# Sample projections in plain fp32 in four column groups from refetched raw weights; the convolution's current-token tap taken by ScalarE from PSUM

## The chip, the core and the metric

One core of one Trainium2 chip runs the whole kernel as one program. The metric is the device time in microseconds (us) of one execution. TensorE (PE) multiplies, VectorE (DVE), ScalarE (ACT) and GpSimd (POOL) do the elementwise work, and SyncE (SP) issues the DMAs, all of them on one queue. Each engine executes its own instruction list in order and waits for the others by semaphores.

## What is computed

One layer of a decoder trunk, for 2048 prompt tokens and for 8 sample tokens (one new token of each of 8 sequences), with the same weights. Everything is fp32.

```
h    = rms_norm(x) * (1 + scale) + shift           # width 1024
proj = h @ w_in                                    # u_a, z_a, q k v, z_b, gates
y_a  = pool_mix(u_a) * silu(z_a)                   # causal pooling, windows 2 4 8 16
q,k,v = silu(causal_conv(qkv))                     # 4 taps per channel
o    = gated delta rule(q, k, v, beta, g)          # chunked for the prompt, one step for the sample
y    = concat(y_a, rms_norm(o) * silu(z_b)) @ w_out
out  = x + gate * rms_norm(y)
```

The convolution of token i is x[i-3]*w[0] + x[i-2]*w[1] + x[i-1]*w[2] + x[i]*w[3]. The part of it that this case touches is the last tap, that of the current token.

## The kernel before

The prompt is worked in four blocks of 512 tokens. In each block PE goes through 24 projection tiles of 128 output channels (tiles 0 to 11 are k, q and v, tiles 12 to 23 are z and u) and then 8 output tiles. Every big product is made of three fp32r products, high x high, high x low and low x high, so a projection tile is 24 matmuls of 128x128 by 128x512 (`tile`, lines 2128 to 2130) into one of two PSUM accumulators, `acc[t % 2]`. Tile t may start when the reader of tile t-2 has emptied that accumulator (`tile_reader`).

The weights come raw from memory only in block 0. There SP loads 256 KB halves into three buffers `wraw`, ACT rounds each half to fp32r (the high part, L901), POOL or DVE subtracts (the low part, L1900), and SP stores the finished 1 MB tile to the DRAM copy `kept`. Blocks 1 to 3 load those 1 MB tiles from `kept` into one of three slots `wsl` (`load_tile`, L739): the load of tile t+3 waits until PE has finished tile t. Since SP runs one list, every wait of SP delays what stands behind it.

A q, k or v tile is convolved after PE: ACT copies the accumulator to `raw` (L934). DVE multiplies `raw` with the first tap into `cacc` (`convolve`, L1248) and adds the other three taps, each with one scalar_tensor_tensor (L1251). ACT then takes the silu into `cq` (L993) and, for q and k, the square into `tmpa` (L1001). `cacc` has two buffers. Between the convolutions DVE builds the gate rows (gg, L1643, which needs ACT's logarithm L1032) that PE waits for behind tile 3, the decay matrices, and from tile 8 on a forward substitution in 31 pairs of small operations (L1333, L1336), before and between the readers of tiles 12 and 13 (L1367).

The 8 sample tokens ride along in block 3, the last one. Ahead of each projection tile PE computes the same 128 channels for them (`sample_tile`): the normed rows are the stationary operand, as fp32r, 16 columns wide (high and low parts of 8 rows, `hs2`), and the tile of weights, already in its slot `wsl`, is the moving one; 16 matmuls of 128 columns (L2204, L2205). ACT copies the 16 rows to `spt`, and after each four tiles PE turns them with four transposes (`sample_join`, L2215) and DVE adds high and low (L1384) into `pj`. From there the sample's convolution, state step and output follow in small steps that ride in the slots behind the projection tiles.

Of the kernel before, what the change touches and what calls it, by code (L numbers as in the profile page):

```python
# [283 lines left out]
def sample_out_steps():  # L284
# [14 lines left out]
    "dve": (["xn", "h0", "h", "hh", "hl"] + ["g_a", "pg0", "g_beta", "g_sp", "g_g", "pg1", "g_d0", "g_d1"] + sample_plan_steps() + sample_out_steps() + ["ys1", "yn", "yr"]),  # L299
# [3 lines left out]
def layer_kernel(nc, a):  # L303
    ctx = ExitStack()
    with ctx:
# [62 lines left out]
        spt = over("spt", rw, 0, [2 * NS, WR, BT])  # L368
# [31 lines left out]
        hs2 = sb("hs2", [P, KT, 2 * NS], F32R)  # L400
# [29 lines left out]
        fold = sb("fold", [GR * BS, 1 + NS])  # L430
# [15 lines left out]
        hs = sb("hs", [P, KT, NS])  # L446
# [113 lines left out]
        raw_f, hist_in, hist_out = event("raw_f", NQ), event("hist_in", NQ), event("hist_out", NQ)  # L560
        conv_a, conv, silu = event("conv_a", 3 * NQ), event("conv", NQ), event("silu", NQ)
# [103 lines left out]
        def tile_reader(eng, it, t):  # L665

            t = t - 2
            if t < 0:
                eng.wait_ge(*ytok_f(it, t - 2))
            elif t < NQ:  # L670
                eng.wait_ge(*raw_f(it, t))
# [16 lines left out]
        def _(sp):  # L688
# [51 lines left out]

            def y_rows(it):

                for t in range(4):
                    sp.wait_ge(*yr_f(it, t))
                    sp.dma_start(a["y"][it, t], ytok[:, t]).then_inc(y_out.sem, 16)
# [17 lines left out]
            def block_of(it, last=False):  # L763
                enter(it)
                if last:
                    sp.wait_ge(*h_hi(it, -1))
                    sp.wait_ge(*h_lo(it, -1))
                    for dst, src in ((cbuf, a["s_conv"]), (pbuf, a["s_pool"])):
                        sp.dma_start(dst[:], src).then_inc(sm_st, 16)
                    sp.dma_start(ssm[:], a["s_ssm"]).then_inc(sm_ssm, 16)  # L770

                for t in range(NW):
                    if it == 0:
                        split_tile(t)
# [99 lines left out]
        def _(act):  # L874
# [96 lines left out]
            def sample_tile(it, t):  # L971

                g, j = divmod(t, 4)
                act.wait_ge(*done("pe", f"sp{t}"))
                if t == 0:
                    act.wait_ge(*split_done(NW - 1, 1))
                if j == 0 and g >= WR:
                    act.wait_ge(*done("pe", f"sc{g - WR}"))
                nc.scalar.activation(spt[:, g % WR, j * P:(j + 1) * P], bank("sp", t)[0:2 * NS, 0:P], ACT.Copy).then_inc(*step("act", f"pj{t}"))
# [166 lines left out]
        def _(dve):  # L1146
# [7 lines left out]
            nc.vector.memset(ones[:], 1.0)  # L1154
            nc.vector.memset(hot[:], 0.0).then_inc(s_pad, 1)
# [84 lines left out]
            def convolve(it, t):  # L1240
# [4 lines left out]
                dve.wait_ge(*raw_f(it, t))  # L1245
                dve.wait_ge(*hist_in(it, t))
                dve.wait_ge(*silu(it, t - 2))
                nc.vector.tensor_scalar(cacc[:, t % 2], r[:, 0:BT], cw[:, t, 0:1], None, ALU.mult).then_inc(conv_a.sem, 1)  # L1248
                for j in range(1, CK):
                    dve.wait_ge(*conv_a(it, 3 * t + j - 1))  # L1250
                    nc.vector.scalar_tensor_tensor(out=cacc[:, t % 2], in0=r[:, j:j + BT], scalar=cw[:, t, j:j + 1],  # L1251
                                                   in1=cacc[:, t % 2], op0=ALU.mult, op1=ALU.add
                                                   ).then_inc((conv_a if j < CK - 1 else conv).sem, 1)
# [121 lines left out]
            def sample_join(it, g):  # L1375
# [4 lines left out]
                turned = bank("sc", g)[:, 0:8 * NS].rearrange("p (t e s) -> p t s e", e=2, s=NS)  # L1380

                def join(to, tiles):

                    return nc.vector.tensor_reduce(pj[:, to:to + tiles.stop - tiles.start], turned[:, tiles], AX.X, ALU.add)  # L1384
# [177 lines left out]
            def sample_rows():  # L1562

                dve.wait_ge(*done("pe", "hs"))
                nc.vector.tensor_tensor(hs[:], row_bank[:, 0:64].rearrange("p (k s) -> p k s", k=KT), amul[:, :, 1:1 + NS],
                                        ALU.mult).then_inc(*step("dve", "h0"))
                dve.wait_ge(*done("dve", "h0"))
                nc.vector.tensor_tensor(hs[:], hs[:], mod[:, 0:8, 1:1 + NS], ALU.add).then_inc(*step("dve", "h"))
                dve.wait_ge(*done("dve", "h"))
                nc.vector.tensor_copy(hs2[:, :, 0:NS], hs[:]).then_inc(*step("dve", "hh"))  # L1570
                dve.wait_ge(*done("dve", "hh"))
                nc.vector.tensor_tensor(hs2[:, :, NS:], hs[:], hs2[:, :, 0:NS].bitcast(F32), ALU.subtract).then_inc(*step("dve", "hl"))
# [19 lines left out]
            def block_of(it, last=False):  # L1592
                enter(it)
                for t in range(NQ):
# [434 lines left out]
        def _(pe):  # L2029
# [15 lines left out]
            def turn_rows(j):  # L2045

                pe.wait_ge(s_rows, j + 1)
                for i in range(4):
                    last = nc.tensor.matmul(turn_bank[j // 2][:, 36 * (j % 2) + 9 * i:36 * (j % 2) + 9 * (i + 1)],
                                            rows96[j][:, i * P:(i + 1) * P], fold[:], start=True, stop=True)  # L2050
# [159 lines left out]
            def sample_join(it, g):  # L2210
# [77 lines left out]
            def block_of(it, last=False):  # L2288
                enter(it)
                for t in range(NQ):  # L2290
                    if last:
                        if t == 0:
                            pe.wait_ge(*done("dve", "hl"))
# [147 lines left out]
def layouts(i):  # L2441
# [5 lines left out]
    def tiles(w):  # L2447
# [20 lines left out]
        "fold": np.tile(np.concatenate([np.eye(1 + NS), np.zeros((BS - 1 - NS, 1 + NS))]), (GR, 1)).astype(np.float32),  # L2468
# [64 lines left out]
```

## Time and profile before

| what | value |
|---|---|
| median of 3 runs | 1063.57 us (1062.31 to 1066.26) |
| profiled execution | 1062.29 us, of it the span of the trace 1060.5 us |
| PE busy | 1017.0 us, 96% of the span |
| DVE, ACT, POOL busy | 669.1, 363.8 and 218.0 us |
| DMA moved | 202.32 MB |
| block 3 begins | 768.81 us after the start |

PE is busy almost throughout, so the columns to look at are how long each piece of its work occupies it (from one start to the next, since matmuls overlap) and the few places where it waits. The other engines' busy time matters only at those places.

### The profile page before, as it was taken

Reading aid. Unit: us, or ns where it says so; the run is one execution under the profiler, and the core shown is the slowest. Engines: PE = TensorE matmul, PEld = TensorE weight load, DVE = VectorE, ACT = ScalarE, POOL = GpSimd, SP = SyncE. Lnnn points to the kernel's source line nnn. Section 1 sums busy time; section 2 is a strip of 40 time slices with the busy share of each in tenths; the row PEclk is TensorE's granted clock in tenths of the full one; section 3 lists DMA queues with packets and bytes.
Section 4 is the critical chain, followed back from the end, with each engine's and each line's share of the span. In section 5 each row is a group of like instructions: output and inputs, shape, how many; then the busy total and the mean of one; then the engine's idle time right before and its main releaser. Section 6 shows DMA issues by size and latency. Waiting matters only on the chain.

```text
span 1060.5 us, 16761 instructions
## 1 busy us (share of the span) xinstructions
PE 1017.0 (96%) x6235; PEld 796.3 (75%) x6235; DVE 669.1 (63%) x1392; ACT 363.8 (34%) x725; POOL 218.0 (21%) x222
## 2 busy tenths in 40 slices
PE   4999989999999999999999999999999999999995
PEld 1567667877777788887877788887877888888774
DVE  2479897577356795566356884676256775555644
ACT  5356322433714511322524511314426531121211
POOL 0133345565400101231000102230000100533000
PEclk9989999999999999999999999999999999999998
DMA  9696566364867553243756553244674343322265
GB/s 344 250 363 230 207 221 269 123 221 160 294 223 269 197 195 128 112 159 132 265 184 252 199 198 120 80 178 160 258 283 169 119 159 120 115 80 86 95 233 179
DMA packets 46803, 202.32 MB, mean 191 GB/s; under 512 B 9162, under 2 KB 9930, under 8 KB 29188
## 3 DMA queue, kind: packets, MB, share of 16 engines
q1 hardware_dynamic: 46724, 201.26, 51.8%
q8 instruction: 50, 0.82, 0.3%
q14 instruction: 29, 0.24, 0.1%
HBM read 156.43 MB, written 44.81 MB: 190 GB/s over the span
## 4 chain that ended last, share of the span: by engine, by line
PE 66%; DVE 1%; issue 1%; POOL 1%; ACT 0%; DVEq 0%; POOLq 0%; ACTq 0%
PE acc L2128 13%; PE acc L2130 12%; PE acc L2129 12%; PE ring L2178 9%; PE ring L2165 2%; PE acc L2165 2%; PE ring L2166 2%; PE ring L2167 2%; PE acc L2167 2%; PE acc L2166 2%; PE ring L2195 1%; PE ring L2204 1%; PE ring L2205 1%; PE ring L2365 1%; PE ring L2187 1%
## 5 line engine op out<-in xcount | busy, mean ns | idle before, releaser
L2128 PE MATMUL acc<-hhi,wsl 128*128 128x512 f32 x768 | 317.8, 414 | 4.8 <-DVE y L1367 4.7
L2130 PE MATMUL acc<-hhi,wsl 128*128 128x512 f32 x768 | 301.7, 393 | 0.0
L2129 PE MATMUL acc<-hlo,wsl 128*128 128x512 f32 x768 | 301.4, 392 | 0.0
L2128 PEld LDWEIGHTS acc<-hhi,wsl 128*128 128x128 f32 x768 | 145.7, 190 | 43.6 <-issue 10.6
L2130 PEld LDWEIGHTS acc<-hhi,wsl 128*128 128x128 f32 x768 | 145.1, 189 | 31.9
L2129 PEld LDWEIGHTS acc<-hlo,wsl 128*128 128x128 f32 x768 | 145.5, 189 | 27.8 <-issue 2.2
L1251 DVE SCALAR_TENSOR_TENSOR cacc<-raw,cw,cacc 128x512 f32<-128x512 f32 x144 | 114.8, 797 | 5.1
L1900 POOL TENSOR_TENSOR wsl<-wraw,wsl 128x512 fp32r<-128x512 f32 x60 | 84.1, 1418 | 107.7 <-ACT wsl L901 107.7
L934 ACT ACTIVATE raw<-acc 128x512 f32<-128x512 f32 x48 | 28.6, 597 | 140.6 <-PE acc L2130 140.5
L2165 PE MATMUL acc<-wsl,yhi 128*128 128x512 f32 x128 | 51.4, 401 | 5.0 <-DVE y L1367 3.4
L1248 DVE TENSOR_SCALAR cacc<-raw,cw 128x512 f32<-128x512 f32 x48 | 25.4, 529 | 47.1 <-ACT raw L934 44.3
L1965 POOL TENSOR_TENSOR on<-on,mhalf 128x4 f32<-128x4 f32 x16 | 23.2, 1447 | 138.8 <-DVE on L1784 138.8
L2165 PE MATMUL ring<-wsl,yhi 128*128 128x512 f32 x128 | 50.6, 396 | 0.4
L901 ACT ACTIVATE wsl<-wraw 128x512 fp32r<-128x512 f32 x64 | 37.8, 621 | 37.2 <-DMA wraw<-in_w 36.4
L2167 PE MATMUL acc<-wsl,yhi 128*128 128x512 f32 x128 | 50.0, 390 | 0.0
L2166 PE MATMUL acc<-wsl,ylo 128*128 128x512 f32 x128 | 49.9, 390 | 0.0
L2167 PE MATMUL ring<-wsl,yhi 128*128 128x512 f32 x128 | 49.9, 390 | 0.0
L2166 PE MATMUL ring<-wsl,ylo 128*128 128x512 f32 x128 | 49.9, 390 | 0.0
L993 ACT ACTIVATE cq<-cacc 128x512 f32<-128x512 f32 x48 | 30.2, 629 | 45.5 <-DVE cacc L1251 45.1
L1091 ACT ACTIVATE junk<-ao 128x128 bf16<-128x128 f32 x64 | 19.9, 310 | 74.4 <-DVE ao L1772 72.9
L942 ACT ACTIVATE tmpa<-acc 128x512 f32<-128x512 f32 x32 | 19.0, 595 | 62.9 <-PE acc L2130 62.5
L1336 DVE TENSOR_TENSOR xt<-xt,stmp 128x126 f32<-128x126 f32 (+22 forms) x124 | 37.7, 304 | 4.3
(323 smaller groups left out, 1668.2 us busy)
## 6 DMA issues: line engine op xcount, KB each, us to landing
wsl<-kept_w SPq DMA_DIRECT2D x96, 1024.0 KB, 4.8
kept_w<-wsl SPq DMA_DIRECT2D x32, 1024.0 KB, 6.5
wraw<-in_w SPq DMA_DIRECT2D x64, 256.0 KB, 4.1
xb<-in_x SPq DMA_DIRECT2D x16, 512.0 KB, 5.7
wada<-in_w_ada SPq DMA_DIRECT2D x8, 1024.0 KB, 11.2
xres<-in_x SPq DMA_DIRECT2D x16, 512.0 KB, 5.7
out_y<-ytok SPq DMA_DIRECT2D x16, 512.0 KB, 8.1
xtr<-in_xt SPq DMA_DIRECT2D x12, 512.0 KB, 7.2
```

Source lines behind the costliest of these rows:

```text
L901: nc.scalar.activation(wsl[:, t % WS, 0, e * (KT // 2):(e + 1) * (KT // 2)], wraw[:, n % WR], ACT.Copy).then_inc(w_hi, 1)
L993: nc.scalar.activation(cq[:, t], cacc[:, t % 2], ACT.Silu).then_inc(silu.sem, 1)
L1251: nc.vector.scalar_tensor_tensor(out=cacc[:, t % 2], in0=r[:, j:j + BT], scalar=cw[:, t, j:j + 1], in1=cacc[:, t % 2], op0=ALU.mult, op1=A ...
L1336: nc.vector.tensor_tensor(xt[:, 0:m, m // 2:], xt[:, 0:m, m // 2:], t, ALU.subtract).then_inc(sub_f.sem, 1)
L1900: nc.gpsimd.tensor_tensor(wsl[:, t % WS, 1, ks], wraw[:, n % WR], wsl[:, t % WS, 0, ks].bitcast(F32), ALU.subtract).then_inc(w_lo, 1)
L2128: nc.tensor.matmul(acc[t % 2][:], w[:, 0, k], hi[:, k], start=(k == 0), stop=False)
L2129: nc.tensor.matmul(acc[t % 2][:], w[:, 0, k], lo[:, k], start=False, stop=False)
L2130: last = nc.tensor.matmul(acc[t % 2][:], w[:, 1, k], hi[:, k], start=False, stop=(k == KT - 1))
L2165: nc.tensor.matmul(o, yhi[:, k, cols], w_hi_k, start=(k == 0), stop=False)
L2166: nc.tensor.matmul(o, ylo[:, k, cols], w_hi_k, start=False, stop=False)
L2167: last = nc.tensor.matmul(o, yhi[:, k, cols], w_lo_k, start=False, stop=(k == KT - 1))
L2178: last = nc.tensor.matmul(bank(kind, i)[rows, h * n:(h + 1) * n], left(h), right(h), start=True, stop=True)
```

## The change

Two edits that don't depend on each other.

**Sample projections.** The rows stay plain fp32 in `hpad` (8 rows in 32 zero-padded columns). A sample tile is 8 fp32 matmuls, 32 stationary columns each, spread over the four 32-column groups of the array, so that the four partial sums land on four groups of PSUM rows. Their moving operand is no longer the slot `wsl` but the raw fp32 tile, fetched again from memory in block 3 into two of the three `wraw` halves. ACT copies 128 rows instead of 16. The join is four fp32 matmuls with the matrix `fold`, which turn and sum the four groups at once; DVE only copies. There is one raw buffer: the fetch for tile t waits for the sample matmuls of tile t-1. The two operations that made `hs2` go.

**Convolution.** In all four blocks ACT makes a second pass over the accumulator, with the last tap as scale, straight into `cacc`; DVE then adds the three older taps. The accumulator is free after the second pass.

```diff
@@ SP
+            def sample_weights(t):
+                if t:
+                    sp.wait_ge(*done("pe", f"sp{t - 1}"))
+                else:
+                    sp.wait_ge(*split_done(NW - 1, 1))
+                for e in range(2):
+                    sp.dma_start(wraw[:, e], a["w"][t][:, e * (KT // 2):(e + 1) * (KT // 2)]).then_inc(raw_in[e], 16)
...
                 if last:
+                    sample_weights(0)
                     sp.wait_ge(*h_hi(it, -1))
...
                     elif t + WS < NW:
+                        if last and t == 0:
+                            sample_weights(1)
+                        if last and t + 2 < OUT:
+                            sample_weights(t + 2)
                         load_tile(it, t + WS)
@@ ACT, tile
                     nc.scalar.activation(raw[:, t % RAW, CK - 1:], acc[t % 2][:], ACT.Copy).then_inc(raw_f.sem, 1)
+                    act.wait_ge(*silu(it, t - 2))
+                    if it == 0 and t == 0:
+                        act.wait_ge(s_prm2, 64)
+                    nc.scalar.activation(cacc[:, t % 2], acc[t % 2][:], ACT.Copy, scale=cw[:, t, CK - 1:CK]).then_inc(raw_f.sem, 1)
@@ ACT, sample_tile
-                nc.scalar.activation(spt[:, g % WR, j * P:(j + 1) * P], bank("sp", t)[0:2 * NS, 0:P], ACT.Copy).then_inc(*step("act", f"pj{t}"))
+                nc.scalar.activation(spt[:, j * P:(j + 1) * P], bank("sp", t)[:, 0:P], ACT.Copy).then_inc(*step("act", f"pj{t}"))
@@ DVE, convolve
-                dve.wait_ge(*silu(it, t - 2))
-                nc.vector.tensor_scalar(cacc[:, t % 2], r[:, 0:BT], cw[:, t, 0:1], None, ALU.mult).then_inc(conv_a.sem, 1)
-                for j in range(1, CK):
-                    dve.wait_ge(*conv_a(it, 3 * t + j - 1))
+                for j in range(CK - 1):
+                    if j:
+                        dve.wait_ge(*conv_a(it, 2 * t + j - 1))
                     nc.vector.scalar_tensor_tensor(out=cacc[:, t % 2], in0=r[:, j:j + BT], scalar=cw[:, t, j:j + 1],
                                                    in1=cacc[:, t % 2], op0=ALU.mult, op1=ALU.add
@@ PE, sample_tile
-                pe.wait_ge(*weights_in(it, t))
                 bank_free(pe, it, "sp", t)
-                w = wsl[:, slot(it, t)]
                 for k in range(KT):
-                    nc.tensor.matmul(bank("sp", t)[0:2 * NS, 0:P], hs2[:, k], w[:, 0, k], start=(k == 0), stop=False)
-                    last = nc.tensor.matmul(bank("sp", t)[0:NS, 0:P], hs2[:, k, 0:NS], w[:, 1, k], start=False, stop=(k == KT - 1))
+                    e, i = divmod(k, KT // 2)
+                    g = k % NBK
+                    if i == 0:
+                        pe.wait_ge(raw_in[e], 16 * (len(range(e, 2 * NW, WR)) + t + 1))
+                    last = nc.tensor.matmul(bank("sp", t)[g * BS:(g + 1) * BS, 0:P], hpad[:, k], wraw[:, e, i],
+                                            start=(k < NBK), stop=(k >= KT - NBK))
@@ PE, sample_join
-                    last = nc.tensor.transpose(bank("sc", g)[:, 2 * j * NS:2 * (j + 1) * NS], spt[:, g % WR, j * P:(j + 1) * P],
-                                               ident[0:2 * NS, 0:2 * NS])
+                    last = nc.tensor.matmul(bank("sc", g)[:, j * NS:(j + 1) * NS], spt[:, j * P:(j + 1) * P], fold[:, 0:NS],
+                                            start=True, stop=True)
```

The order of instructions moves at three places. The first is SP's list where block 3 begins: the three loads into the slots that end the list of block 2, then the sample's states. Before:

```order
L739 DMA wsl<-kept_w 128x2048 [waits proj] x3
L769 DMA cbuf<-in_s_conv 128x288 [waits h_lo,h_hi]
L769 DMA pbuf<-in_s_pool 128x480
L770 DMA ssm<-in_s_ssm 128x4096
L739 DMA wsl<-kept_w 128x2048 [waits proj] x2
L745 DMA out_y<-ytok 128x1024 [waits yr_f] x4
```

And of the changed kernel, the same place:

```order
L739 DMA wsl<-kept_w 128x2048 [waits proj] x3
L748 DMA wraw<-in_w 128x512 [waits w_lo]
L748 DMA wraw<-in_w 128x512
L779 DMA cbuf<-in_s_conv 128x288 [waits h_lo,h_hi]
L779 DMA pbuf<-in_s_pool 128x480
L780 DMA ssm<-in_s_ssm 128x4096
L748 DMA wraw<-in_w 128x512 [waits sample_pe]
L748 DMA wraw<-in_w 128x512
L748 DMA wraw<-in_w 128x512 [waits sample_pe]
L748 DMA wraw<-in_w 128x512
L739 DMA wsl<-kept_w 128x2048 [waits proj]
```

The first raw tile stands behind the last of the three slot loads, which waits for PE's last output tile of block 2; each later one waits for the sample matmuls one tile earlier and stands ahead of a slot load.

The second is PE's list at the same place, the first sample tile of block 3 and the first matmul of projection tile 0. Before:

```order
L2204 MATMUL ring<-wsl,hs 16x128 [waits w_in0,ya_f,s_pre,sample_dve]
L2205 MATMUL ring<-wsl,hs 8x128
L2204 MATMUL ring<-wsl,hs 16x128
L2205 MATMUL ring<-wsl,hs 8x128
...
L2128 MATMUL acc<-hhi,wsl 128x512 [waits h_lo,ytok_f,w_in0]
```

And of the changed kernel:

```order
L2222 MATMUL ring<-wraw,hpad 32x128 [waits ya_f,raw_in0,s_pre,sample_dve]
L2222 MATMUL ring<-wraw,hpad 32x128 x3
L2222 MATMUL ring<-wraw,hpad 32x128 [waits raw_in1]
L2222 MATMUL ring<-wraw,hpad 32x128 x3
L2144 MATMUL acc<-hhi,wsl 128x512 [waits h_lo,ytok_f,w_in0]
```

Eight matmuls stand where sixteen stood, and they wait for the raw halves (raw_in0, raw_in1) instead of the slot (w_in0).

The third is ACT's list in block 0 around tiles 1 and 2, with the chain to the logarithm that the gate rows need. Before:

```order
L934 ACTIVATE raw<-acc 128x512 [waits hist_out,conv,proj]
L993 ACT_TABLE_LOAD [waits proj]
L993 ACTIVATE cq<-cacc 128x512 [waits conv]
L1001 ACTIVATE tmpa<-cq 128x512 [waits z_f,silu]
L1024 ACTIVATE btt<-btt 128x16 [waits dve_factors]
L901 ACTIVATE wsl<-wraw 128x512 [waits w_kept1,proj,raw_in2]
L901 ACTIVATE wsl<-wraw 128x512 [waits raw_in0]
L934 ACTIVATE raw<-acc 128x512 [waits hist_out,conv,proj]
L993 ACTIVATE cq<-cacc 128x512 [waits conv]
```

And of the changed kernel:

```order
L948 ACTIVATE raw<-acc 128x512 [waits hist_out,conv,proj]
L952 ACTIVATE cacc<-acc,cw 128x512 [waits silu]
L1011 ACT_TABLE_LOAD [waits proj]
L1011 ACTIVATE cq<-cacc 128x512 [waits conv]
L1019 ACTIVATE tmpa<-cq 128x512 [waits z_f,silu]
L1042 ACTIVATE btt<-btt 128x16 [waits dve_factors]
L915 ACTIVATE wsl<-wraw 128x512 [waits w_kept1,proj,raw_in2]
L915 ACTIVATE wsl<-wraw 128x512 [waits raw_in0]
L948 ACTIVATE raw<-acc 128x512 [waits hist_out,conv,proj]
L952 ACTIVATE cacc<-acc,cw 128x512 [waits silu]
L1011 ACTIVATE cq<-cacc 128x512 [waits conv]
```

One activation more stands behind each copy to `raw`, ahead of the silu of the tile before.

## Rows read from the trace of the kernel before

**Rows 1.** The page, part 1: busy time of each engine.
```profile
PE 1017.0 (96%) x6235; PEld 796.3 (75%) x6235; DVE 669.1 (63%) x1392; ACT 363.8 (34%) x725; POOL 218.0 (21%) x222
```

**Rows 2.** The waits of PE: total us, times, longest us.
```profile
PE acc L2128 <- DVE y L1367: 4.7, 2, 3.1
```

**Rows 3.** Timeline of PE, one sample tile: start us, duration us, count.
```profile
778.71 0.39 PE L2138 MATMUL ring<-hlo,wg 128*16 128x512 f32 x1
778.94 0.22 PE L2204 MATMUL ring<-wsl,hs 128*16 128x128 f32 x1
...
779.90 0.45 PE L2128 MATMUL acc<-hhi,wsl 128*128 128x512 f32 x1
```

**Rows 4.** Timeline of PE: four fp32 matmuls in four column groups.
```profile
807.75 0.39 PE L2130 MATMUL acc<-hhi,wsl 128*128 128x512 f32 x1
808.07 0.42 PE L2334 MATMUL ring<-tmpa,hot 128*32 128x128 f32 x8
808.42 0.50 PE L2347 MATMUL ring<-grow,gpick 48*128 48x512 f32 x1
```

**Rows 5.** Timeline of PE: 32 fp32 matmuls (64 records) in four column groups.
```profile
899.11 1.94 PE L2260 MATMUL ring<-ssm,km 128*16 128x128 f32 x64
900.98 0.50 PE L2128 MATMUL acc<-hhi,wsl 128*128 128x512 f32 x1
```

**Rows 6.** Timeline of PE: one join of four sample tiles.
```profile
802.04 0.42 PE L2215 MATMUL ring<-ident,spt 16*128 16x16 f32 x4
802.38 0.50 PE L2128 MATMUL acc<-hhi,wsl 128*128 128x512 f32 x1
```

**Rows 7.** Timeline of PE: four fp32 matmuls, 128 stationary columns (8 records).
```profile
986.19 1.03 PE L2276 MATMUL ring<-pls,poolw 128*128 128x8 f32 x8
987.08 0.36 PE L2178 MATMUL ring<-ub,mt 128*128 128x128 f32 x1
```

**Rows 8.** Timeline of SP where block 3 begins: issue time, us.
```profile
769.00 0.32 SPq L739 DMA_DIRECT2D wsl<-kept_w  x1
769.42 0.38 SPq L769 DMA_DIRECT2D cbuf<-in_s_conv  x1
```

**Rows 9.** DMA issues: count, KB each, median us to landing.
```profile
wsl<-kept_w SPq DMA_DIRECT2D x96, 1024.0 KB, 4.8
...
wraw<-in_w SPq DMA_DIRECT2D x64, 256.0 KB, 4.1
...
cbuf<-in_s_conv SPq DMA_DIRECT2D x1, 144.0 KB, 4.8
```

**Rows 10.** Window 771 to 774: busy us, PEclk, DMA share, GB/s.
```profile
771.00:774.00 3.00, 3.00 (x15) 2.49 (x14) 2.68 (x3) 0.00 (x0) 0.38 (x2) 1.00 0.96 389
```

**Rows 11.** Windows of block 0, the same columns (PE, PEld, DVE, ACT, POOL).
```profile
64.00:68.80 4.80, 2.89 (x15) 1.93 (x13) 4.16 (x11) 4.74 (x8) 1.76 (x2) 1.00 0.99 326
68.80:75.60 6.80, 6.80 (x25) 5.25 (x25) 5.42 (x10) 2.88 (x5) 3.55 (x3) 0.50 0.96 345
112.80:153.10 40.30, 34.58 (x164) 24.22 (x162) 37.99 (x76) 13.40 (x26) 17.76 (x13) 1.00 0.49 174
149.00:154.10 5.10, 1.97 (x9) 1.33 (x8) 5.00 (x6) 2.07 (x4) 4.38 (x4) 1.00 0.60 195
154.10:157.50 3.40, 3.40 (x10) 2.62 (x9) 3.13 (x9) 0.63 (x1) 1.58 (x2) 0.50 1.01 377
```

**Rows 12.** Groups by line: busy us, mean ns of one.
```profile
L934 ACT ACTIVATE raw<-acc 128x512 f32<-128x512 f32 x48 | 28.6, 597 | 140.6 <-PE acc L2130 140.5
...
L1248 DVE TENSOR_SCALAR cacc<-raw,cw 128x512 f32<-128x512 f32 x48 | 25.4, 529 | 47.1 <-ACT raw L934 44.3
```

**Rows 13.** Timelines of ACT, DVE and PE: the gate chain of block 0.
```profile
66.23 0.22 ACT L1032 ACTIVATE gl<-gl 128x16 f32<-128x16 f32 x1
...
67.16 1.20 DVE L1643 TENSOR_TENSOR gg<-gsp,vec 128x48 f32<-128x48 f32 x1
...
68.42 0.42 PE L2318 MATMUL ring<-upper,gg 128*48 128x128 f32 x2 [1.91 <-DVE gg L1643]
```

More of the change, by code:

```diff
@@ L298 @@
     "pool": ["rx0", "rx", "clear", "half", "rk", "rstd", "ry0", "ry"],
-    "dve": (["xn", "h0", "h", "hh", "hl"] + ["g_a", "pg0", "g_beta", "g_sp", "g_g", "pg1", "g_d0", "g_d1"] + sample_plan_steps() + sample_out_steps() + ["ys1", "yn", "yr"]),
+    "dve": (["xn", "h0", "h"] + ["g_a", "pg0", "g_beta", "g_sp", "g_g", "pg1", "g_d0", "g_d1"] + sample_plan_steps() + sample_out_steps() + ["ys1", "yn", "yr"]),
 }
@@ L367, in layer_kernel @@
         wraw = over("wraw", rw, 0, [P, WR, KT // 2, P])
-        spt = over("spt", rw, 0, [2 * NS, WR, BT])
+        spt = over("spt", rw, 4 * KB, [P, BT])
         xb = over("xb", re_, 24 * KB, [P, 4, DM])
@@ L399, in layer_kernel @@
         cin = over("cin", rs, KB, [P, KT, 1 + NS])
-        hs2 = sb("hs2", [P, KT, 2 * NS], F32R)
+        hpad = sb("hpad", [P, KT, BS])
         ym2 = sb("ym2", [P, 8, 2 * NS], F32R)
@@ L429, in layer_kernel @@
         rows96 = [t[0:GR * BS, j] for t in (tmpa, pooled) for j in range(2)]
-        fold = sb("fold", [GR * BS, 1 + NS])
+        fold = sb("fold", [P, 1 + NS])
         ssx = sb("ssx", [P, 4]); rx0 = sb("rx0", [P, 4]); rx = sb("rx", [P, 4])
@@ L443, in layer_kernel @@
         oss = sb("oss", [P, H]); on0 = sb("on0", [P, H]); on = sb("on", [P, H])
-        hs = sb("hs", [P, KT, NS])
+        hs = hpad[:, :, 0:NS]
         g8, s8 = sb("g8", [NS, 8, H]), sb("s8", [NS, 8])
@@ L559, in layer_kernel @@
         proj = event("proj", NW)
-        raw_f, hist_in, hist_out = event("raw_f", NQ), event("hist_in", NQ), event("hist_out", NQ)
-        conv_a, conv, silu = event("conv_a", 3 * NQ), event("conv", NQ), event("silu", NQ)
+        raw_f, hist_in, hist_out = event("raw_f", 2 * NQ), event("hist_in", NQ), event("hist_out", NQ)
+        conv_a, conv, silu = event("conv_a", 2 * NQ), event("conv", NQ), event("silu", NQ)
         sq = event("sq", 8)
@@ L670, in tile_reader @@
             elif t < NQ:
-                eng.wait_ge(*raw_f(it, t))
+                eng.wait_ge(*raw_f(it, 2 * t + 1))
             else:
@@ L976, in sample_tile @@
                     act.wait_ge(*split_done(NW - 1, 1))
-                if j == 0 and g >= WR:
-                    act.wait_ge(*done("pe", f"sc{g - WR}"))
-                nc.scalar.activation(spt[:, g % WR, j * P:(j + 1) * P], bank("sp", t)[0:2 * NS, 0:P], ACT.Copy).then_inc(*step("act", f"pj{t}"))
+                if j == 0 and g:
+                    act.wait_ge(*done("pe", f"sc{g - 1}"))
+                nc.scalar.activation(spt[:, j * P:(j + 1) * P], bank("sp", t)[:, 0:P], ACT.Copy).then_inc(*step("act", f"pj{t}"))
             def head_row(it, n):
@@ L1154, in _ @@
             nc.vector.memset(ones[:], 1.0)
+            nc.vector.memset(hpad[:], 0.0)
             nc.vector.memset(hot[:], 0.0).then_inc(s_pad, 1)
@@ L1379, in sample_join @@
                     dve.wait_ge(*h_lo(it, -1))
-                turned = bank("sc", g)[:, 0:8 * NS].rearrange("p (t e s) -> p t s e", e=2, s=NS)
+                turned = bank("sc", g)[:, 0:4 * NS].rearrange("p (t s) -> p t s", s=NS)
                 def join(to, tiles):
-                    return nc.vector.tensor_reduce(pj[:, to:to + tiles.stop - tiles.start], turned[:, tiles], AX.X, ALU.add)
+                    return nc.vector.tensor_copy(pj[:, to:to + tiles.stop - tiles.start], turned[:, tiles])
                 if g < 4:
@@ L1564, in sample_rows @@
                 dve.wait_ge(*done("pe", "hs"))
-                nc.vector.tensor_tensor(hs[:], row_bank[:, 0:64].rearrange("p (k s) -> p k s", k=KT), amul[:, :, 1:1 + NS],
+                nc.vector.tensor_tensor(hs, row_bank[:, 0:64].rearrange("p (k s) -> p k s", k=KT), amul[:, :, 1:1 + NS],
                                         ALU.mult).then_inc(*step("dve", "h0"))
                 dve.wait_ge(*done("dve", "h0"))
[L1568 to L1572, printed above, removed]
+                nc.vector.tensor_tensor(hs, hs, mod[:, 0:8, 1:1 + NS], ALU.add).then_inc(*step("dve", "h"))
                 dve.wait_ge(s_const, 64)
@@ L1593, in block_of @@
                 enter(it)
+                if it == 0:
+                    dve.wait_ge(s_prm2, 64)
                 for t in range(NQ):
@@ L2049, in turn_rows @@
                     last = nc.tensor.matmul(turn_bank[j // 2][:, 36 * (j % 2) + 9 * i:36 * (j % 2) + 9 * (i + 1)],
-                                            rows96[j][:, i * P:(i + 1) * P], fold[:], start=True, stop=True)
+                                            rows96[j][:, i * P:(i + 1) * P], fold[0:GR * BS], start=True, stop=True)
                 last.then_inc(s_tr, 1)
@@ L2292, in block_of @@
                         if t == 0:
-                            pe.wait_ge(*done("dve", "hl"))
+                            pe.wait_ge(*done("dve", "h"))
                             pe.wait_ge(s_pre, 3)
@@ L2467, in layouts @@
         "gsel": pick,
-        "fold": np.tile(np.concatenate([np.eye(1 + NS), np.zeros((BS - 1 - NS, 1 + NS))]), (GR, 1)).astype(np.float32),
+        "fold": np.tile(np.concatenate([np.eye(1 + NS), np.zeros((BS - 1 - NS, 1 + NS))]), (NBK, 1)).astype(np.float32),
         "c_all": np.concatenate([f("c_prompt"), f("c_sample")]).T.reshape(KT, P, 1 + NS).transpose(1, 0, 2),
```

4 lines of the change are left out of this document (2 added, 2 removed).

## The prediction

> **What bounds the kernel now.** I read the page first: PE is busy 96% of the span, DVE 63%, ACT 34% [rows 1]. So a microsecond counts where PE works less or more, and at the few places where PE waits. The waits of PE come next. Behind the first loads, the largest is on DVE, 4.7 us in two stretches at L2128, the longest 3.1 us [rows 2]; both lie in block 0, at the starts of tiles 14 and 15, which need DVE to have read tiles 12 and 13 out of the accumulators. Another 1.9 us, also in block 0, is the wait for the gate rows gg [rows 13]. In blocks 1 to 3 the projection tiles hardly wait. Last I read windows around those waits for the granted clock: it is 0.50, the 1.2 GHz level, from 68.8 to 75.6 and from 154.1 to 157.5, in each case just after PE had been idle [rows 11]. Half the clock for 6.8 and 3.4 us costs 3.4 and 1.7 us.
>
> So the change must be priced at three places: PE's sample work in block 3, the start of block 3, and DVE's convolutions in block 0.
>
> **A. The sample tiles, on PE.** A sample tile now occupies PE from 778.94 to 779.90, 0.96 us, with 0.23 us between the start of the matmul ahead and its first [rows 3]. No row has the new form, 8 fp32 matmuls of 32 stationary and 128 moving columns. Its nearest relative is the four-matmul sum over heads: 0.35 us from its start to the next instruction, and 0.32 us instead of 0.23 ahead of it [rows 4]. Thirty-two such matmuls on the same four groups take 1.87 us, 0.058 each [rows 5]. Four more matmuls are thus 0.23 us, and the new tile is 0.09 + 0.35 + 0.23 = 0.67 us, 0.29 less. Over 24 tiles that is -7.0 us. Ten of the 24 follow other fp32 work directly and don't pay the 0.09, -0.9. The lower bound of the gain is twice rows 4 (0.79 us a tile, -4.1 in all), the upper one rows 5 alone (0.47 us, -11.8).
>
> The 0.09 us ahead of a group and the 0.20 behind it (the last of the 1.87 us) are where a rule speaks against this change. In the Trainium skill, "TensorEngine Tiling (Array Packing)", section "Key Properties", changing the tiling mode drains the engine. It names no price. The rows above agree with a small one; were each of the two switches of a tile a drain of 0.42 us, the length of the four-matmul group in rows 4, a tile would take 0.84 + 4 x 0.11 = 1.3 us and the 24 would lose 8 us instead of winning 7. My sum goes by the rows.
>
> **B. The joins, on PE.** Four transposes take 802.04 to 802.38, 0.34 us [rows 6]. Four fp32 matmuls with 128 stationary columns and 8 moving ones take 986.19 to 987.08, 0.89 us [rows 7]. Six joins cost 6 x 0.55 = +3.3 us. Together A and B give -4.6.
>
> **C. The first fetch.** This is the large new cost. PE goes from the last output tile of block 2 straight into sample tile 0, at 768.81, since the weights have long been in a slot. In the changed kernel SP issues the fetch for sample tile 0 behind the last slot load, which itself waits for that last output tile: it leaves at 769.00, and at 769.42, where cbuf stands now, the first raw half [rows 8]. cbuf, 144 KB behind 1 MB, landed 4.8 us after its issue, at 774.2 [rows 9]. The half has 256 KB, 112 more at 389 GB/s [rows 10], so 774.5, and the second half follows 0.7 us later, 775.2. With the last four matmuls and the switch tile 0 starts at 775.5. Without the wait it would start at 768.81 + 0.67 = 769.5: +6.0 us of PE idle. Lower bound: the median 4.1 us of a lone 256 KB half and 0.7, +5.0; upper: the 1.5 MB at half that rate, 4 us more, +10. Nothing hides it; the tiles behind it can't go ahead. PE's later fetches are cheaper: the one for tile t leaves when the sample matmuls of t-1 end, 24 matmuls of 0.23 us = 5.5 us before it is wanted, and lands 4.1 + 0.7 = 4.8 us later. The one for tile 1 stands behind the 2 MB of ssm, but tile 0 is followed by 16 gate matmuls of 0.23 us, 3.7 us. The slot loads come 0.7 us later behind them and have two tiles to spare.
>
> **D. The clock behind that stall.** Idle stretches of 1.9 us, up to 68.4 [rows 13], and of 3.1 us, up to 153.1 [rows 2], were followed by 6.8 and 3.4 us at 1.2 GHz [rows 11]. Six us idle should do it too: I take the shorter, 3.4 us at half, +1.7; bounds 0 and +3.4. The Trainium skill, "TensorE: Matmul & The Clock Gate", section "What's actually happening", says the same way round that the throttled state is the default and activity releases it. By it too the stall costs more than its length.
>
> **E. The gate chain of block 0.** gg ends at 68.36 and PE starts at 68.42 [rows 13]. Ahead of gg stand DVE's convolutions of tiles 0 to 2, each one pass of 529 ns shorter [rows 12], -1.6, and the two dropped sample operations. The other branch, ACT's logarithm, ends 0.7 us before gg starts; it gets two passes of about 0.6 us [rows 12] in front but its own start moves with DVE. I take -1.6; bounds -1.9 (PE no longer waits) and +0.6 (ACT's branch decides).
>
> **F. The DVE-bound stretch of block 0.** From 112.8 to 153.1 DVE is busy 38.0 of 40.3 us [rows 11], and PE waits for its end. The convolutions of tiles 7 to 11 stand in or right ahead of it: 5 x 0.53 = -2.7 us, of the 4.7 us that PE waits [rows 2]. ACT's second pass runs while DVE substitutes, so it is hidden: ACT is busy 13.4 us of that stretch. Bounds 0 and -4.7. In blocks 1 to 3 DVE's shorter list meets no wait of PE, 0; ACT's longer one has a whole tile (5.5 us) to be hidden behind, four passes in it being 2.5 us.
>
> Sum: -4.6 + 6.0 + 1.7 - 1.6 - 2.7 = -1.2 us, on the profiled execution's 1062.3, so 1061.1. That execution lies 1.3 us under the median of the runs, 1063.6, and from the median the sum is 1062.4. I say 1061.5.
>
> **The rivals.**
>
> *The clock holds in block 0* (0.22). E and F shorten just those idle stretches that the two drops of the clock follow [rows 11]. If PE stays warm at both, 3.4 + 1.7 = 5.1 us come on top: 1056.4. For it: the wait up to 68.4 shrinks from 1.9 to about 0.3. Against: 2.0 us would remain of the two waits at tiles 14 and 15.
>
> *ACT passes the delay on* (0.16). If the second pass holds ACT's list up as much as DVE's gets shorter (DVE waits 44.3 us for ACT's raw as it is, rows 12), E and F give nothing: 1061.5 + 4.3 = 1065.8. This is the case that half of the change doesn't do what it says.
>
> *Each refetch is late* (0.12). The spare time is 5.5 against 4.8 us. It is gone when the raw halves have to share the queue with a slot load: 1 MB at 389 GB/s is 2.7 us, so 7.5 against 5.5, up to 2 us a tile for the 12 tiles at the front of block 3; those from 12 on have other work between. Half of that, 1 us a tile, is +12: 1073. Against it: a raw tile is issued ahead of the slot load of its step, and 1.5 MB take 3.9 us of at least 5.5. It decides from a landing of about 6 us on.
>
> The forecast itself has 0.45, with 1058 to 1065 as its own range; 0.05 is left for others.
>
> **How the numbers follow.** Within 0.5% (5.3 us, about what a measurement of this kernel can tell from no change) of 1063.6 is 1058.3 to 1068.9. Faster: most of the first rival and the lower end of the forecast, 0.29. Slower: the third rival and a little, 0.13. The same: 0.58. The range takes in the first rival and the second and stops short of the third: 1055 to 1068.
>
> **What would show it.** A sample tile that takes 0.6 to 0.7 us from start to next start (A), joins of 0.9 (B). PE idle from 768 to 774 or so, with the DMA of wraw as what ends it, and PEclk 0.50 behind it (C, D). L2144's wait for DVE y at 2 us instead of 4.7, and gg's under 1 us (E, F). The prediction is wrong if waits for wraw stand at more than two or three sample tiles, if PE starts block 3 without a gap, or if both drops of the clock in block 0 are gone.

## The result: 0.5% slower, outside the range of the prediction

The changed kernel takes 1069.84 us (median of 4 runs, 1067.94 to 1070.97) against 1063.95 us of the kernel before (4 runs, 1062.31 to 1066.26). The ratio is 1.0052, with a 95% interval of 1.0029 to 1.0075. The forecast was 1061.5, the range ended at 1068.

The profiled execution of the changed kernel took 1067.94 us, with a span of 1066.2. From its page come the busy times, and after them a few of PE's waits (total us, times, longest us).

```profile
PE 1017.5 (95%) x6259; PEld 787.7 (74%) x6259; DVE 643.8 (60%) x1343; ACT 391.4 (37%) x773; POOL 219.1 (21%) x222
```

```profile
PE ring L2222 <- DMA wraw<-in_w: 7.8, 2, 5.9
...
PE acc L2144 <- DVE y L1385: 2.6, 1, 2.6
PE ring L2336 <- DVE gg L1659: 1.3, 1, 1.3
...
PE ring L2233 <- ACT spt L997: 1.0, 1, 1.0
```

DVE lost 25 us of work and ACT gained 28, as the change says [rows 1]. PE's busy time looks unchanged, which will turn out to be two things that cancel. The wait for y went from 4.7 to 2.6 us [rows 2], the one for gg from 1.9 to 1.3 [rows 13]. Two new kinds of wait have come, both in block 3: wraw at L2222 (the sample tiles), and ACT's copy spt at L2233 (a join).

Where is the time, then? I cut the span where the last output matmul of block 2 starts: 768.58 us before, 762.64 after. Here are the windows from that cut to the end, before first, then after (the columns as in rows 10).

```profile
768.58:1060.50 291.92, 279.12 (x1955) 222.34 (x1953) 172.94 (x399) 77.06 (x173) 41.91 (x43) 0.99 0.41 149
```

```profile
762.64:1066.20 303.56, 281.70 (x1979) 215.94 (x1977) 167.51 (x387) 84.27 (x185) 41.85 (x43) 0.96 0.52 185
```

So blocks 0 to 2 are 5.9 us shorter and block 3 is 11.6 us longer, with the granted clock down from 0.99 to 0.96. The timeline of PE and that of ACT show three stops in block 3 (start us, duration, idle before and its releaser). I call the time from the start of the matmul ahead to the start behind a stop the start gap; without a stop it is 0.2 to 0.3 us. The first is at sample tile 0:

```profile
762.64 0.39 PE L2183 MATMUL ring<-wsl,yhi 128*128 128x512 f32 x1
768.97 1.21 PE L2222 MATMUL ring<-wraw,hpad 128*32 128x128 f32 x16 [5.94 <-DMA wraw<-in_w]
```

The second is at sample tile 4, and the third at the third join, where ACT makes both passes over the stream's tile before the copy that the join needs:

```profile
801.38 0.43 PE L2352 MATMUL ring<-tmpa,hot 128*32 128x128 f32 x8
803.62 1.26 PE L2222 MATMUL ring<-wraw,hpad 128*32 128x128 f32 x16 [1.82 <-DMA wraw<-in_w]
...
865.83 0.64 PE L2222 MATMUL ring<-wraw,hpad 128*32 128x128 f32 x16
867.43 0.92 PE L2233 MATMUL ring<-fold,spt 128*128 128x8 f32 x7 [0.95 <-ACT spt L997]
```

```profile
865.94 0.60 ACT L948 ACTIVATE raw<-acc 128x512 f32<-128x512 f32 x1 [2.73 <-PE acc L2146]
866.43 0.68 ACT L952 ACTIVATE cacc<-acc,cw 128x512 f32<-128x512 f32 x1
867.00 0.28 ACT L997 ACTIVATE spt<-ring 128x128 f32<-128x128 f32 x1
```

With each of the three goes a stretch at a granted clock of 0.50, the 1.2 GHz level. The first begins inside the stop, while PE is idle, the other two behind it. These windows show them:

```profile
766.10:772.90 6.80, 3.93 (x23) 2.65 (x24) 4.22 (x5) 0.00 (x0) 0.00 (x0) 0.50 1.03 413
803.60:810.40 6.80, 6.78 (x33) 5.24 (x34) 2.28 (x6) 0.96 (x3) 0.00 (x0) 0.50 0.70 237
868.50:871.90 3.40, 3.40 (x9) 2.63 (x9) 0.00 (x0) 0.88 (x3) 0.00 (x0) 0.50 0.82 273
```

Half the clock costs half of the busy time in such a window: 2.0, 3.4 and 1.7 us. The starts that the stops put off are 6.1, 1.9 and 1.1 us late. Together that is 16.2 us, against about 4.1 us that the shorter sample work saves (measured below), so +12.1 where the windows say +11.6. The loss is accounted for to half a microsecond, but by reading one execution; the experiments test it.

Why is tile 4 late? SP's timeline and, under it, the landings of what was issued from 789.3 to 791.5 and from 794 to 796 us (count, KB, median us to landing):

```profile
789.39 3.57 SPq L754 DMA_DIRECT2D out_y<-ytok  x4
794.93 0.84 SPq L748 DMA_DIRECT2D wraw<-in_w  x2
795.82 0.46 SPq L739 DMA_DIRECT2D wsl<-kept_w  x1
```

```profile
out_y<-ytok SPq DMA_DIRECT2D x4, 512.0 KB, 9.9
...
wraw<-in_w SPq DMA_DIRECT2D x2, 256.0 KB, 8.7
```

The refetch of tile 4 stands behind the four output rows of block 2, 2 MB, and takes 8.7 us to land. The median of all 112 fetches of wraw is 3.6. A 1 MB slot load, issued at 788.91, stands just ahead of the rows. The last row lands at 802.8, the two halves of the refetch at 803.5 and 804.2. From the first row's issue to the refetch's, the queue moved less than the 389 GB/s of [rows 10]:

```profile
789.39:794.93 5.54, 5.54 (x60) 4.31 (x59) 1.91 (x9) 1.70 (x6) 0.00 (x0) 1.00 0.89 253
```

### The profile page after: what moved, and what is told of

The parts are those of the page before. It is cut to its first block, busy times and chain, and to the rows that moved or that the text cites. A ratio compares the mean times of both kernels' runs of the same rounds, so it can differ in the third digit from the quotient of the medians.

```text
span 1066.2 us, 16859 instructions
## 1 busy us (share of the span) xinstructions
PE 1017.5 (95%) x6259; PEld 787.7 (74%) x6259; DVE 643.8 (60%) x1343; ACT 391.4 (37%) x773; POOL 219.1 (21%) x222
## 4 chain that ended last, share of the span: by engine, by line
PE 78%; DVE 6%; DMA 5%; issue 4%; POOL 2%; ACT 2%; SPq 1%; DVEq 0%; ACTq 0%; POOLq 0%
PE acc L2144 15%; PE acc L2145 14%; PE acc L2146 14%; PE ring L2194 11%; DMA wraw<-in_w 4%; PE ring L2181 2%; PE acc L2181 2%; PE ring L2182 2%; PE ring L2183 2%; PE acc L2183 2%; PE acc L2182 2%; PE ring L2211 2%; PE ring L2383 1%; PE ring L2222 1%; DVE cacc L1269 1%
## 5 line engine op out<-in xcount | busy, mean ns | idle before, releaser
L1351 DVE TENSOR_TENSOR stmp<-lb,xt 128x126 f32<-128x126 f32 (+22 forms) x124 | 36.5, 294 | 3.6
```

Of the source, the lines that this page charges most:

```text
L1351: nc.vector.tensor_tensor(t, lb[:, m, 0:m].unsqueeze(2).to_broadcast([P, m, n]), xt[:, m, m // 2:].unsqueeze(1).to_broadcast([P, m, n]), A ...
```

## The experiments

All times are medians in us; a ratio is that to the kernel before on the same chip, with its 95% interval. Kernel 1 is the kernel of experiment 1, and so on. My theory after the result: the two halves of the change work as priced, and the stops of PE in block 3, with the clock behind them, lose more than they gain. The rivals: the clock falls because the new sample work itself keeps TensorE less busy; or the refetches' traffic slows everything; or the new sample tiles gain nothing.

**1. The convolution's part alone** (e1_conv_only). The sample's tiles, joins and loads are those of the kernel before. Of the diff the ScalarE pass and VectorE's shorter loop are left:

```diff
+                    act.wait_ge(*silu(it, t - 2))
+                    nc.scalar.activation(cacc[:, t % 2], acc[t % 2][:], ACT.Copy, scale=cw[:, t, CK - 1:CK]).then_inc(raw_f.sem, 1)
...
-                nc.vector.tensor_scalar(cacc[:, t % 2], r[:, 0:BT], cw[:, t, 0:1], None, ALU.mult).then_inc(conv_a.sem, 1)
-                for j in range(1, CK):
+                for j in range(CK - 1):
```

> The kernel before with the convolution edit alone. My theory: the edit gives the 5.9 us by which block 3 began earlier in the changed kernel (762.9 against 768.8), and nothing in blocks 1 to 3, so about 1058 us, 0.5 to 0.6% less than before. The rival, that ACT's second pass costs as much in blocks 1 to 3 as DVE's shorter list gives in block 0, says 1062 to 1065.

Measured: 1060.39 against 1064.22, ratio 0.9961 (0.9942 to 0.9979). That is between my theory (1058) and the rival (1062 or more). The forecast for E and F was -4.3 us; the medians say -3.8. Block 3 takes 292.5 us from the cut, 0.6 more than before. There is one new wait in it, at the third join, whose transposes now wait for ACT's copy:

```profile
860.38 0.39 PE L2220 MATMUL ring<-ident,spt 16*128 16x16 f32 x4 [0.54 <-ACT spt L983]
```

So ScalarE's second pass by itself delays block 3 by about half a microsecond.

**2. The sample's part alone** (e2_sample_only). The convolution is that of the kernel before.

```diff
-                    nc.scalar.activation(cacc[:, t % 2], acc[t % 2][:], ACT.Copy, scale=cw[:, t, CK - 1:CK]).then_inc(raw_f.sem, 1)
...
+                nc.vector.tensor_scalar(cacc[:, t % 2], r[:, 0:BT], cw[:, t, 0:1], None, ALU.mult).then_inc(conv_a.sem, 1)
```

> The kernel before with the sample edit alone. My theory: all of the 11.6 us by which block 3 grew from its first instruction to the end (from 291.7 to 303.3 us) comes from this edit, less the wait of the third join, which needs ACT's second pass as well (1.0 us and the 1.7 us of a slow clock behind it): 1072 to 1076 us. The rival, that both edits load ACT and PSUM together and that either alone costs little, says under 1070.

Measured: 1071.55 against 1064.22, ratio 1.0056 (1.0033 to 1.0079). That is half a microsecond under the range of my theory and well over the rival. It stops at sample tile 0 (start gap 6.07 us) and at tile 4 (1.84), each with 6.8 us at 0.50. The trace names VectorE's gd for tile 4, but the first raw half landed at the same moment, 0.1 us ahead of PE's start. At the third join the wait is only 0.4 us. The two parts' ratios multiply to 1.0017, 0.35% under the whole change's 1.0052, 3.7 us. The third join's stop with its clock is 2.8 us in the whole change, and comes to that size in neither part alone (0.5 and 0.4 us of wait, no 0.50 behind it). It takes a shorter sample tile (join reached sooner) and a longer ACT list (copy made later). That the 3.7 us are this interaction isn't shown: the intervals are as wide as it is.

**3. The first refetch earlier** (e3_first_early). It is issued in block 2, at the step of the first output tile.

```diff
                 if last:
-                    sample_weights(0)
                     sp.wait_ge(*h_hi(it, -1))
...
+                    if it == LAST - 1 and t == OUT:
+                        sample_weights(0)
```

> The changed kernel with only the first refetch moved, to the middle of block 2's list, behind projection tile 24's step, so that it has landed long before block 3. My theory: the 6.1 us of PE idle and the 2.0 us of the slow clock behind it go, so 8 us less than the changed kernel, 1061 to 1063 us. The rival, that the queue is the limit and the wait only moves to the next refetches, says less than 3 us, 1067 or more.

Measured: 1063.33, ratio 0.9993 (0.9975 to 1.0012). The stop at tile 0 is gone, and 0.6% (6.3 us) with it, where I expected 8. A part came back at tile 1: its refetch stands right behind the 2 MB of ssm and lands 9.9 us after its issue, and 3.4 us at 0.50 follow. PE's timeline:

```profile
772.44 0.39 PE L2155 MATMUL ring<-hlo,wg 128*16 128x512 f32 x1
774.89 0.96 PE L2223 MATMUL ring<-wraw,hpad 128*32 128x128 f32 x16 [2.06 <-DMA wraw<-in_w]
```

**4. The output rows one a step** (e4_spread_y). Kernel 3, with the four rows of out_y each behind that step's refetch and slot load.

```diff
-                    if t == 1 and it:
+                    if t == 1 and it and not last:
                         y_rows(it - 1)
+                    if last and 1 <= t < 5:
+                        sp.wait_ge(*yr_f(it - 1, t - 1))
+                        sp.dma_start(a["y"][it - 1, t - 1], ytok[:, t - 1]).then_inc(y_out.sem, 16)
```

> The former with block 2's output rows issued one a step at tiles 1 to 4 of block 3, each behind the refetch and slot load of its step, where all four (2 MB) stood ahead of the refetch for sample tile 4. My theory: that refetch was late because of the 2 MB, so the 1.9 us wait at sample tile 4 goes and the clock doesn't fall to 0.50 behind it (3.4 us): 5 us less than the former, 1056 to 1058 us. A rival says that the sample work in four column groups is too little for the clock and that it falls around there without an idle stretch too: 2 us less, 1060.

Measured: 1056.98, ratio 0.9930 (0.9906 to 0.9954): faster than before by 0.7%. The wait at tile 4 is gone. Its front, from the first sample tile to the first state update, has a granted clock of 1.00:

```profile
761.44:889.57 128.13, 125.44 (x905) 95.40 (x904) 79.20 (x204) 55.88 (x104) 4.84 (x5) 1.00 0.72 246
```

That settles two rivals. The four-column work is all in there, PE is busy in 98% of the window, and the clock holds; and the refetches' traffic is all there too, 246 GB/s, and nothing but the stops named next comes of it. Two stops remain in the window, 2.04 us (start gap) at tile 1 and 1.22 at the third join. After neither did the clock fall in this execution.

**5. The copy ahead of the passes** (e5_copy_first). Kernel 4, with ACT's copy of the sample tile in front.

```diff
-                    tile(it, t)
                     if last:
                         sample_tile(it, t)
+                    tile(it, t)
```

> e4_spread_y with ACT's copy of a sample tile put ahead of its two passes over the projection tile of the same step; the sample tile is done on PE before that projection tile. My theory: the third join waited 1.0 us for that copy because it stood behind raw and cacc, so it no longer waits: 1 us less than e4, plus up to 1.7 us in executions where the clock fell behind it, about 1055 to 1056 us. The rival, that the join waits for its own PSUM bank or for DVE, leaves the gap of 1.2 us at the third join.

Measured: 1058.67, ratio 0.9958 (0.9942 to 0.9973). The join no longer waits, yet the time isn't lower than kernel 4's; the intervals overlap. In its profiled execution the stop at tile 1 was 2.53 us and was followed by 3.4 us at 0.50, which kernel 4's was not. This run doesn't show a gain from the copy; I had expected 1055 to 1056.

**6. The sample's states later** (e6_states_later). Kernel 5, with cbuf, pbuf and ssm issued at step 6 of block 3, out of the way of the refetch of tile 1.

```diff
                 for t in range(NW):
+                    if last and t == 6:
+                        for dst, src in ((cbuf, a["s_conv"]), (pbuf, a["s_pool"])):
+                            sp.dma_start(dst[:], src).then_inc(sm_st, 16)
+                        sp.dma_start(ssm[:], a["s_ssm"]).then_inc(sm_ssm, 16)
```

> The former with the sample's states (2.4 MB) issued at step 6 of block 3 instead of ahead of the second refetch. My theory: sample tile 1 waits 2.0 us in e3 and e4 because its refetch stands behind them; the wait goes, and then PE has no wait for wraw in block 3 and the clock stays at 1.00 through it although all the sample work is in four column groups: 2 us less, 1053 to 1054 us. The rival, that the sample work itself lowers the clock, shows a window at 0.50 in block 3 all the same.

Measured: 1055.87 against 1062.66, ratio 0.9935 (0.9917 to 0.9953); I had expected 1053 to 1054. No wait for wraw over 0.8 us is left and no clock under 1.00 in the front, which takes 126.6 us:

```profile
766.46:893.06 126.60, 125.61 (x904) 95.32 (x904) 79.24 (x204) 56.12 (x104) 4.84 (x5) 1.00 0.72 249
```

**7. The wait alone** (e7_wait_only). Kernel 1, which has the old sample tiles, fetches one raw tile where the change puts its first refetch, and PE waits for it ahead of sample tile 0. Nothing uses the tile.

```diff
                 if last:
+                    sp.wait_ge(*split_done(NW - 1, 1))
+                    for e in range(2):
+                        sp.dma_start(wraw[:, e], a["w"][0][:, e * (KT // 2):(e + 1) * (KT // 2)]).then_inc(raw_in[e], 16)
...
                         if t == 0:
+                            for e in range(2):
+                                pe.wait_ge(raw_in[e], 16 * (len(range(e, 2 * NW, WR)) + 1))
```

> The kernel of e1 (convolution edit alone, sample tiles from the slots) with one raw tile fetched where the changed kernel fetches its first, and PE's first sample tile waiting for it without using it. It prices the first wait by itself. My theory: 6 us of idle and 2 to 3.4 us of a slow clock behind it, 8 to 9 us over e1, 1068 to 1070 us. The rival, that part of the stall is given back because DVE, ACT and the slot loads catch up meanwhile, says 4 us or less over e1.

Measured: 1068.56, ratio 1.0049 (1.0028 to 1.0070). Against kernel 1 (ratio 0.9961) that is 0.9%, 9.3 us by the ratios, 8.2 by the medians. The timeline of PE and the window of the clock:

```profile
767.25 0.39 PE L2175 MATMUL ring<-wsl,yhi 128*128 128x512 f32 x1
774.01 0.27 PE L2212 MATMUL ring<-wsl,hs 128*16 128x128 f32 x1 [6.37 <-DMA wraw<-in_w]
```

```profile
771.00:777.80 6.80, 3.79 (x21) 3.43 (x22) 3.94 (x5) 0.00 (x0) 0.00 (x0) 0.50 1.04 425
```

The start is put off by 6.5 us and half of the 3.79 us of work at 0.50 is 1.9: 8.4 us, and its block 3 is 8.3 us longer than kernel 1's (300.8 against 292.5). The clock falls here before any sample work has run, in an idle stretch behind old fp32r matmuls, so that stretch is enough, whatever the sample tiles are made of.

**8 and 9. One cure at a time, on the changed kernel itself** (e8_rows_only, e9_copy_only). The first has only the edit of kernel 4, the second only that of kernel 5; the first refetch stays where the change put it.

> The changed kernel, with the output rows of block 2 issued one a step at steps 1 to 4 of block 3, each behind that step's refetch; the first refetch stays where the change put it. Theory (the late refetch of sample tile 4 is a price of its own: 1.9 us of wait and 3.4 us of the 6.8 us at a granted clock of 0.50 behind it): about 5 us less than the changed kernel's 1069.8, 1065; sample tile 0 still waits about 6 us. Rival (the wait at sample tile 0 delays everything and the second wait only takes slack that was there): 1069 to 1070.

> The changed kernel, with ScalarE's copy of a sample tile ahead of its two passes over the stream's tile in the front of block 3. Theory (the third join waits for that copy behind the second pass, 1.1 us, and the clock falls after it, 1.7 us): 1067, no start gap over 0.5 us at the third join, no granted clock of 0.50 behind it, the stops at sample tiles 0 and 4 as before. Rival (what the copy gains the passes lose, and VectorE's convolution then comes late for TensorE): 1069 to 1071 with a new wait for xv or y behind the front.

Measured: with the rows spread 1063.81, ratio 0.9991 (0.9975 to 1.0007), 0.6% or 6.5 us under the changed kernel's ratio, where the theory had 5 and the rival 0. Of its stops, 6.19 us at tile 0 is still there and the one at tile 4 is not: the second wait was a price of its own. The third join still waits 0.9 us in its trace, and no 0.50 follows it. The two cures add up: 0.59% for the first refetch alone (kernel 3), 0.61% for the rows alone, 1.22% for both (kernel 4). With the copy ahead 1068.77, ratio 1.0037 (1.0015 to 1.0059). The third join no longer waits:

```profile
864.50 0.64 PE L2222 MATMUL ring<-wraw,hpad 128*32 128x128 f32 x16
865.08 1.06 PE L2233 MATMUL ring<-fold,spt 128*128 128x8 f32 x8
865.99 0.48 PE L2144 MATMUL acc<-hhi,wsl 128*128 128x512 f32 x1
```

The idle is gone and no 0.50 stands behind it, but 0.15% is less than the 2.8 us (0.26%) that I expected and less than the intervals can tell from nothing. The trace is of an execution of 1064.01, 4.8 us under the median: in it the stop at tile 4 was short as well (start gap 1.23) and no 0.50 followed it either. So it can't say what the copy is worth. The size of that third price is open.

**10 and 11. What the new sample tiles are worth without the stops** (e10_old_sample, e11_new_sample). Kernel 10 is kernel 1 with the three order edits of 4, 5 and 6. Kernel 11 is kernel 6 again, to stand on the same chip as kernel 10. Their difference is the sample's arithmetic, joins and refetches.

> The convolution's part of the change alone, with the order of the experiments before it (output rows one a step, the sample's states at step 6, the copy ahead of the passes), and the sample's tiles in fp32r from the slots as in the kernel before. Theory A (the fp32 column groups save what the sum gave them, 7.9 us less 3.3 at the joins): 3 to 4.6 us over the kernel with the new sample tiles that runs beside it, near 1060. Theory B (the gain of those experiments came from their order alone, the arithmetic gives nothing net): within 1 us of it, near 1056.

> The same program as e6_states_later (both parts of the change, first refetch in block 2, output rows one a step, states at step 6, the copy ahead of the passes), on the same chip as e10_old_sample, to be compared with it. Theory A: 1056, 3 to 4.6 us under e10_old_sample. Theory B: equal to e10_old_sample within 1 us.

Measured: 1059.07, ratio 0.9960 (0.9946 to 0.9975), and 1057.18, ratio 0.9940 (0.9925 to 0.9956). Kernel 10 equals kernel 1 (0.9961), so the order edits give nothing that can be measured without the new tiles. The new tiles give 1.9 us, between the two theories (3 to 4.6, and less than 1); the six runs of each hardly overlap (1058.4 to 1060.3, 1055.1 to 1059.1), but the two intervals overlap. The windows from the end of block 2, of kernel 10 and then of kernel 11, say where:

```profile
764.62:1056.60 291.98, 279.16 (x1955) 222.31 (x1953) 167.28 (x387) 84.43 (x185) 41.95 (x43) 0.99 0.42 149
```

```profile
766.91:1055.80 288.89, 275.01 (x1979) 211.59 (x1977) 167.58 (x387) 84.46 (x185) 41.92 (x43) 0.99 0.55 192
```

PE is busy 4.15 us less, of the 4.6 that A and B forecast, and block 3 is 3.1 us shorter, in part because a late refetch remains at tile 8 (it now stands behind ssm):

```profile
831.40 0.86 PE L2227 MATMUL ring<-wraw,hpad 128*32 128x128 f32 x12 [0.67 <-DMA wraw<-in_w]
```

Blocks 0 to 2 took 2.3 us longer in kernel 11's profiled execution, although they have the same program but for one early fetch, so these two executions differ by 0.8 us only. Why the medians differ by 1.9 and not by 3.1 isn't shown. Taking the raw tiles' late refetches out altogether, by using the slots' weights in four column groups, wasn't tried.

## Why the prediction was wrong

**A, the sample tiles: right.** A tile follows the matmul ahead after 0.32 us and takes 0.58 to the next:

```profile
780.41 0.39 PE L2154 MATMUL ring<-hlo,wg 128*16 128x512 f32 x1
780.73 0.64 PE L2222 MATMUL ring<-wraw,hpad 128*32 128x128 f32 x16
781.31 0.50 PE L2144 MATMUL acc<-hhi,wsl 128*128 128x512 f32 x1
```

With the 0.09 us ahead that is the 0.67 forecast, and the drains of 0.42 us that I weighed against it are not there.

**B, the joins: right.** 840.03 to 840.95 is 0.92 us, 0.9 forecast:

```profile
840.03 1.06 PE L2233 MATMUL ring<-fold,spt 128*128 128x8 f32 x8
840.95 0.48 PE L2144 MATMUL acc<-hhi,wsl 128*128 128x512 f32 x1
```

Together they measured -4.15 against -4.6, by PE's busy time in kernels 10 and 11.

**C, the first fetch: right.** +6.1 against +6.0, and kernel 7 shows it apart from everything else. **D, the clock behind it: right in mechanism and size**, 2.0 against 1.7, though by luck: it lasted 6.8 us rather than 3.4, but nearly half of that lay in the idle time. The Trainium skill, "TensorE: Matmul & The Clock Gate", section "What's actually happening", has the throttled state as the default that activity releases; the windows agree in that each of the three stretches at 0.50 lies at a stop and at no place where PE worked through.

**The step that failed is the last part of C**: "PE's later fetches are cheaper". I worked out 5.5 us of notice against 4.8 us of landing, and checked what stands in the queue ahead of the fetch for tile 1, but of no other. The four output rows of block 2 are issued at step 1, 5.5 us ahead of the refetch for tile 4 and behind a 1 MB slot load, and the refetch lands after 8.7 us instead of 4.8. Listing the rows wouldn't have been enough. At the 389 GB/s of [rows 10] their 2 MB take 5.4 us and would have been gone when the refetch left, and even with the slot load and the refetch ahead of it the queue would have been empty by about 797.5. It wasn't before 802.8: the rate was 253 GB/s from the first row to the refetch. Why it was lower there isn't shown; that the rows make the refetch late is, by kernels 4 and 8. I named the condition in the third rival ("decides from a landing of about 6 us on") and looked only for slot loads as what could make it true. The case that came is that rival at one tile of twelve, with 1.9 us of wait and 3.4 us of clock, which the rival left out. Kernel 8 measured its removal at 6.5 us by the ratios.

**A smaller step failed in F**: ACT's longer list "has a whole tile (5.5 us) to be hidden behind". Its copy of a sample tile stood behind the second pass, and that copy has no tile of slack, since the join follows it at once. By the profile this is 1.1 us and 1.7 of clock. With the old sample tiles the same wait is 0.5 us in kernels 1 and 7 and gone in kernel 10, which has the copy ahead, so the order of ACT's list is its cause; its worth in time kernel 9 couldn't confirm.

**E and F, block 0: right in sum, and by luck.** -4.3 forecast, -3.8 measured by kernel 1. F holds: the wait for y is 4.7 us in the two kernels without the convolution edit (before and kernel 2), and 2.6 or 2.7 in nine of the eleven with it, 2.1 less against 2.7 forecast (kernels 3 and 9 have 4.0 and 3.9). E isn't shown: gg waits 1.9 and 0.8 us in the two kernels without the edit and 1.0 to 2.0 in those with it. What filled E's place is a wait that I hadn't listed, of the sums over heads for ACT's square of a convolved tile:

```profile
114.76 0.43 PE L2334 MATMUL ring<-tmpa,hot 128*32 128x128 f32 x8 [1.09 <-ACT tmpa L1001]
```

It is there in both kernels without the edit (1.1 and 1.3 us) and in none with it. That a shorter convolution lets ACT begin sooner fits this, but no run tests it by itself. In the two profiled executions, 2.1 for y, 0.6 for gg, 1.1 for this one and 3.4 of clock, less a start of the projections that came 1.2 us later, make the 5.9. The clock was at 0.50 for 10.2 us in block 0 before [rows 11] and for 3.4 after, so my first rival came true in half in this execution. Among the eleven kernels with the edit it was between 0 and 13.6 us. The clock of block 0 differs from one execution to the next, and the medians are what to believe.

Sum: -1.2 forecast, and the two failed steps add 1.9 + 3.4 + 1.1 + 1.7 = 8.1 us: 6.9, with 5.9 measured.

The best orders tried keep both parts of the change and beat both kernels: kernel 4 with 0.9930 of the time before, and kernel 6, which is also 11, with 0.9935 and 0.9940. The intervals don't tell them apart.

## What to carry to other kernels

When a change turns data that lay ready into data that is fetched again just before use, list every transfer in the queue ahead of each fetch, stores of the block before included, and compare bytes over the measured rate with the notice that each fetch has. Take the rate from a stretch with the same mix of loads and stores: here it was 253 GB/s where another stretch had 389. Price a stop of a busy PE with the clock behind it: here up to 3.4 us behind a wait of 1.9. When one engine gets a pass more, look at each thing that it does between that pass and a short-notice reader, not at its busy share.

## What was unexpected of the hardware

The length of a stop didn't decide whether the granted clock fell. A start gap of 1.22 us at the third join was followed by 3.4 us at 0.50 in the changed kernel and kernel 3, and by none in kernels 4 and 8; gaps of 2.09 and 1.95 us at tile 4 were followed by 6.8 us in the changed kernel and in kernel 3, one of 2.04 us at tile 1 of kernel 4 by nothing. Gaps of over 6 us came with 6.8 us at 0.50 in all five kernels that had one, and in each the fall began inside the gap. What else decides it stays open; with such chances of 1.7 to 3.4 us each, single executions of one kernel differ by up to 14.5 us (kernel 9: 1058.92 to 1073.40), and only many runs tell orders apart.
